# Attention rewritten: token-major queries, joined softmax weights, an fp32 V product, all query units ahead of the first score

## The chip, the cores and the metric

The kernel runs on one core of one Trainium2 chip. The metric is device time in microseconds (us): the median of several runs. The engines in the text are TensorE (PE, its weight loads PEld), VectorE (DVE), ScalarE (ACT), GpSimd (POOL) and SyncE (SP, which issues the loads). They run their own instruction lists in order and meet only at semaphores (`wait_ge`).

## The reference

A two-layer decoder trunk on 512 tokens of 1024 features, all float32: a gated short convolution layer, then one layer of differential attention, each with a squared-ReLU MLP. The change lies in the attention. Cut to it:

```python
def diff_attention(h, k, v, w_q, q_norm, lq1, lk1, lq2, lk2, sub_norm, w_o, lam_init):
    q = rms_norm((h @ w_q).reshape(b, s, N_HEADS, 2, HEAD_DIM), q_norm)   # 8 heads, 2 x 64
    lam = ...                                                              # a scalar
    for i in range(s // Q_BLOCK):                                          # 4 blocks of 128 rows
        sc = jnp.einsum('bqhcd,bkhcd->bhcqk', qb, kb) * HEAD_DIM ** -0.5
        p = jax.nn.softmax(jnp.where(causal, sc, NEG_INF), axis=-1)
        a = p[:, :, 0] - lam * p[:, :, 1]
        outs.append(jnp.einsum('bhqk,bkhe->bqhe', a, vb))                  # V_DIM = 128
    o = rms_norm(jnp.concatenate(outs, axis=1), sub_norm) * (1.0 - lam_init)
    return o.reshape(b, s, N_HEADS * V_DIM) @ w_o
```

## The kernel before

**Products.** Every large product is made of three fp32r matmuls: high part times high part, high times low, low times high. ACT makes the high part of a weight slab (`split`, L775) and DVE the low part (L1031). A slab is 512 KB of weights, loaded by SP into one of two raw buffers, and its two parts lie in rings of four. A slab is 24 matmuls of 512 columns (`product`, L436).

**Order.** First layer, its MLP, then 16 slabs of K and V (L585, token-major: four token blocks share a slab), with K normed and transposed head by head (`transpose_k`, L564). Then attention over 8 heads, the output projection (8 slabs), and the second MLP.

**Attention.** Queries are projected feature-major, one slab per head, and two heads ahead: `project` is cut in three pieces, which stand in PE's list between the groups of the head at work. The scale of the queries' norm is not applied to q: sums of q² are made on PE (`head_sums`, L599), POOL takes the power (L367), and exp gets it as its scale, with a bias that DVE makes from the row maximum (L1254, L1256). Each head has four block rows. For each: `scores` (L615, six matmuls, with a mask added at L618), row maximum on DVE, two exps on ACT (L918), the joined weights on DVE in three operations (L1264, L1266, L1268: both softmaxes are scaled, then added), transposes on PE (`weights_T`, L628), and a split of the transposed weights in high part (ACT, L926) and low part (DVE, L1273). The V product (`values`, L642) takes two block rows together, feature-major, in three fp32r terms. Then sums of o² on PE (`out_sums`, L649), the power on POOL (L375), a spread of the scale over the partitions on PE (`out_spread`, L461), the product on DVE (L1284), high part on ACT (L947) and low part on POOL (L400). POOL also makes the low parts of K (L384) and V (L396). Six pieces of the output projection fill PE's list in the last two heads.

Of the kernel before, what the change touches and what calls it, by code (L numbers as in the profile page):

```python
# [19 lines left out]
F32 = mybir.dt.float32  # L20
# [6 lines left out]
P = 128  # L27
T = 512
# [17 lines left out]
B_Q, B_AT, B_O, B_BC = 4, 5, 6, 7  # L46
HEAD_AHEAD = 2
Q_BANK = (B_AT, B_Q)
KV_BANKS = 6
K_T_AFTER = 7  # L50
# [25 lines left out]
def slot(n):  # L76


    return (n % 2) if S_Q <= n < S_WO else n % RING


def freed(n):

    if S_Q + 2 <= n < S_WO + 2:
        return n - 1
    return n - RING + 1 if n >= RING else 0
# [5 lines left out]


def heads(engine, head):


    head(0, 0, None, 1, 2)
    head(1, 1, 0, 2, 3)
    with engine.Fori(0, (H - 4) // 2) as it:
        head(it * 2 + 2, 0, it * 2 + 1, it * 2 + 3, it * 2 + 4)  # L100
        head(it * 2 + 3, 1, it * 2 + 2, it * 2 + 4, it * 2 + 5)
    head(H - 2, 0, H - 3, H - 1, None)
    head(H - 1, 1, H - 2, None, None)


def build(nc, x, a_norm, a_w_in, a_conv, a_w_out, kv_norm, w_kv, k_norm, b_norm, w_q, q_norm,
          lam_q1, lam_k1, lam_q2, lam_k2, sub_norm, w_o, mlp_norm, w_up, w_down, out):
    with ExitStack() as ctx:
# [21 lines left out]
        comp2 = sb("comp2", [P, 2])  # L130
# [12 lines left out]
        qms = sb("qms", [P, 2, 8])  # L143
        qpw = sb("qpw", [P, 8])
        k_ms = sb("k_ms", [P, 2, 32])
        k_rs = sb("k_rs", [P, 2, 32])
        q_scale = sb("q_scale", [P, 2, 2 * TB])
        oms = sb("oms", [P, 8])
        ors = sb("ors", [P, 8])
        nmax = sb("nmax", [P, 2, 2])  # L150
        bias = sb("bias", [P, 2, 2])
        rsum = sb("rsum", [P, 2, 2])
# [9 lines left out]
        p_buf = [work[:, (4 + 2 * i) * T:(6 + 2 * i) * T].rearrange("p (c k) -> p c k", c=2) for i in range(2)]  # L162
        at_hi = [ah[:, 0, :].rearrange("p (j q) -> p j q", j=2), ah[:, 2:4, :].rearrange("p a (j q) -> p (a j) q", j=2)]
        at_lo = [ah[:, 1, :].rearrange("p (j q) -> p j q", j=2), ah[:, 4:6, :].rearrange("p a (j q) -> p (a j) q", j=2)]
        q_hi, q_lo = [ah[:, 6 + 2 * b, :] for b in range(2)], [ah[:, 7 + 2 * b, :] for b in range(2)]
        k_hi, k_lo = [ah[:, 10 + 2 * b, :] for b in range(2)], [ah[:, 11 + 2 * b, :] for b in range(2)]
        v_hi, v_lo = ah[:, 14, :].rearrange("p (t e) -> p t e", t=TB), ah[:, 15, :].rearrange("p (t e) -> p t e", t=TB)
# [6 lines left out]
        sq_q = [work[:, T:2 * T], work[:, 3 * T:4 * T]]  # L174
# [39 lines left out]
        s_kT = sem("s_kT")  # L214
        s_kg = sem("s_kg")
        s_qsq = sem("s_qsq")
# [15 lines left out]
        s_Thi = sem("s_Thi")  # L232
        s_Tlo = sem("s_Tlo")
# [25 lines left out]
        def _(sp):  # L259
# [62 lines left out]
            for h in range(H):  # L322
                load(S_Q + h, cols(wq_d, h))
# [11 lines left out]
        def _(pool):  # L335
# [1030 lines left out]
```

## Time and profile before

| what | value |
|---|---|
| median of 3 runs | 1162.5 us (1161.51 to 1162.87) |
| profiled execution | 1161.75 us, span 1160.0 us |
| granted TensorE clock, mean | 0.999 of full |
| PE busy | 1148.7 us (99%) |
| DVE busy | 632.7 us (55%) |
| ACT busy | 383.2 us (33%) |
| POOL busy | 119.0 us (10%) |

The span goes from the first to the last instruction on the chip. Busy time is summed over instructions of an engine; matmuls overlap one another, so a matmul's own duration is longer than the distance from its start to that of the next.

### The profile page before, as it was taken

The numbers are of one execution on the slowest core, as the hardware profiler recorded it, in microseconds if no ns is written. First come the engines' busy times: TensorE is split into PE (matmuls) and PEld (weight loads), VectorE is DVE, ScalarE is ACT, GpSimd is POOL, SyncE is SP. The second block draws the span as 40 slices with busy tenths as digits, with TensorE's granted clock in tenths as the row PEclk, the third lists the DMA queues.
The fourth block names the chain that finished last, engine by engine and source line by source line (L and its number), as shares of the span: only waits on it lengthen the run. The fifth ranks groups of instructions, "written<-read, shape, count | busy, mean of one in ns | idle before, by whom it ended". The sixth has DMA issues, their size and how long they took to land.

```text
span 1160.0 us, 14437 instructions
## 1 busy us (share of the span) xinstructions
PE 1148.7 (99%) x5448; PEld 948.8 (82%) x5448; DVE 632.7 (55%) x871; ACT 383.2 (33%) x591; POOL 119.0 (10%) x94
## 2 busy tenths in 40 slices
PE   9999999999999999999999999999999999999998
PEld 7788888888888888888888788788888888888887
DVE  5765654733633633655543799946644544544542
ACT  6222133321321321334432677734321221222221
POOL 0000012000000000012210355424000000000000
PEclk9999999999999999999999999999999999999999
DMA  7333333333333333333222101113333233233232
GB/s 182 92 101 104 91 94 106 91 104 96 92 103 97 90 101 97 91 91 110 91 91 73 56 24 32 37 54 99 103 109 109 73 109 109 72 108 109 73 97 85
DMA packets 203109, 105.77 MB, mean 91 GB/s; under 512 B 12592, under 2 KB 198960, under 8 KB 203056
## 3 DMA queue, kind: packets, MB, share of 16 engines
q1 hardware_dynamic: 202016, 105.03, 31.7%
q8 instruction: 36, 0.59, 0.2%
q10 hardware_dynamic: 1040, 0.00, 0.0%
q14 instruction: 17, 0.14, 0.0%
HBM read 102.93 MB, written 2.10 MB: 91 GB/s over the span
## 4 chain that ended last, share of the span: by engine, by line
PE 95%; DVE 2%; issue 1%; DMA 1%; ACT 1%; SPq 0%; ACTq 0%; DVEq 0%
PE ps L436 81%; PE ps L585 8%; PE ps L615 1%; PE ps L642 1%; PE ps L461 1%; PE ps L628 1%; DMA kv<-in_x 1%; PE ps L649 0%; PE ps L618 0%; PE ps L599 0%; DVE nmax L1254 0%; DVE work L1266 0%; PE ps L564 0%; DVE ah L1273 0%; PE ps L553 0%
## 5 line engine op out<-in xcount | busy, mean ns | idle before, releaser
L436 PE MATMUL ps<-h,w_hi 128*128 128x512 f32 x1792 | 556.0, 391 | 1.7 <-DVE w_lo L1031 1.7
L436 PEld LDWEIGHTS ps<-h,w_hi 128*128 128x128 f32 x1792 | 333.3, 188 | 69.9 <-issue 1.6
L436 PE MATMUL ps<-h,w_lo 128*128 128x512 f32 x896 | 349.1, 390 | 0.0
L436 PE MATMUL ps<-ah,w_hi 128*128 128x512 f32 x1024 | 316.0, 390 | 0.0
L775 ACT ACTIVATE w_hi<-w_raw 128x1024 fp32r<-128x1024 f32 x184 | 192.4, 1052 | 253.4 <-DMA w_raw<-in_w_up 113.7
L1031 DVE TENSOR_TENSOR w_lo<-w_raw,w_hi 128x1024 fp32r<-128x1024 f32 x184 | 231.6, 1262 | 55.2 <-ACT w_hi L775 54.4
L436 PEld LDWEIGHTS ps<-ah,w_hi 128*128 128x128 f32 x1024 | 191.8, 188 | 39.8
L436 PE MATMUL ps<-ah,w_lo 128*128 128x512 f32 x512 | 199.3, 389 | 0.0
L436 PEld LDWEIGHTS ps<-h,w_lo 128*128 128x128 f32 x896 | 168.2, 188 | 35.5
L1042 DVE TENSOR_TENSOR xT<-ps,xT 128x512 f32<-128x512 f32 x80 | 55.3, 691 | 205.3 <-PE ps L436 205.3
L854 ACT ACTIVATE ah<-work 128x512 fp32r<-128x512 f32 x64 | 40.5, 633 | 238.8 <-DVE work L1138 238.8
L436 PEld LDWEIGHTS ps<-ah,w_lo 128*128 128x128 f32 x512 | 96.1, 188 | 19.9
L1138 DVE SCALAR_TENSOR_TENSOR work<-ps,rB 128x512 f32<-128x512 f32 x64 | 44.2, 691 | 124.0 <-PE ps L436 118.1
L355 POOL TENSOR_TENSOR work<-work 128x512 f32<-128x512 f32 x24 | 32.2, 1343 | 504.8 <-ACT work L784 504.8
L585 PE MATMUL ps<-w_hi,h 128*128 128x512 f32 x256 | 81.5, 393 | 0.0
L585 PEld LDWEIGHTS ps<-w_hi,h 128*128 128x128 f32 x256 | 48.1, 188 | 9.9
L585 PE MATMUL ps<-w_lo,h 128*128 128x512 f32 x128 | 49.8, 389 | 0.0
L1143 DVE TENSOR_TENSOR ah<-work,ah 128x512 fp32r<-128x512 f32 x64 | 44.4, 693 | 2.7
L1140 DVE TENSOR_TENSOR work<-work 128x512 f32<-128x512 f32 x64 | 44.3, 692 | 2.2
L778 ACT ACTIVATE h<-xT,gains 128x512 fp32r<-128x512 f32 x32 | 23.0, 720 | 65.1 <-DVE xT L1042 65.1
L918 ACT ACTIVATE work<-ps,bias,q_scale 128x128 f32<-128x128 f32 (+3 forms) x64 | 39.2, 627 | 4.2 <-DVE bias L1256 4.2
L1036 DVE SCALAR_TENSOR_TENSOR h<-xT,gains,h 128x512 fp32r<-128x512 f32 x32 | 24.0, 750 | 20.7 <-ACT h L778 20.7
(114 smaller groups left out, 655.1 us busy)
## 6 DMA issues: line engine op xcount, KB each, us to landing
w_raw<-in_w_up SPq DMA_DIRECT2D x64, 512.0 KB, 4.0
w_raw<-in_w_down SPq DMA_DIRECT2D x64, 512.0 KB, 3.8
w_raw<-in_a_w_in SPq DMA_DIRECT2D x23, 512.0 KB, 3.7
w_raw<-in_w_kv SPq DMA_DIRECT2D x16, 512.0 KB, 3.5
w_raw<-in_a_w_out SPq DMA_DIRECT2D x8, 512.0 KB, 3.9
w_raw<-in_w_q SPq DMA_DIRECT2D x8, 512.0 KB, 3.9
w_raw<-in_w_o SPq DMA_DIRECT2D x8, 512.0 KB, 4.0
kv<-in_x SPq DMA_DIRECT2D x4, 512.0 KB, 6.6
```

What stands on the lines that cost most here:

```text
L355: nc.gpsimd.tensor_tensor(sqsum, sqsum, sqb[m % 2], ALU.add).then_inc(s_add, 1)
L436: last = nc.tensor.matmul(ps[:, bank, :], w[:, s, k * P:(k + 1) * P], src(half, k), start=(k == 0 and i == 0), stop=(k == KC - 1 and i == 2))
L585: last = nc.tensor.matmul(ps[:, use % KV_BANKS, :], h2[:, half, k, t * P:(t + 1) * P], w[:, s, k2 * T:(k2 + 1) * T], start=(k == 0 and i = ...
L775: nc.scalar.activation(w_hi[:, slot(n), :], w_raw[:, n % RAW, :], ACT.Copy).then_inc(s_whi, 1)
L854: nc.scalar.activation(ah[:, jj, :], mix[jj % 2], ACT.Square).then_inc(s_ahi, 1)
L918: nc.scalar.activation(p_buf[i % 2][:, c, 0:kw], ps[:, 2 * (i % 2) + c, 0:kw], ACT.Exp, bias=bias[:, i % 2, c:c + 1], scale=q_scale[:, b, ...
L1031: V.tensor_tensor(w_lo[:, slot(n), :], w_raw[:, n % RAW, :], w_hi[:, slot(n), :].bitcast(F32), ALU.subtract).then_inc(s_wlo, 1)
L1036: V.scalar_tensor_tensor(h_of[i][:, 1, m, :], xT[:, m, :], gains[:, g, m:m + 1], h_of[i][:, 0, m, :].bitcast(F32), ALU.mult, ALU.subtract) ...
L1042: V.tensor_tensor(xT[:, m, :], ps[:, bank, :], xT[:, m, :], ALU.add).then_inc(s_acc, 1)
L1138: V.scalar_tensor_tensor(mix[j % 2], ps[:, (ubase + j) % ACC, :], 0.0, rB[:], ALU.max, ALU.mult).then_inc(s_r, 1)
L1140: V.tensor_tensor(mix[2], mix[j % 2], mix[j % 2], ALU.mult).then_inc(s_acc, 1)
L1143: V.tensor_tensor(ah[:, 8 + j, :], mix[2], ah[:, j, :].bitcast(F32), ALU.subtract).then_inc(s_alo, 1)
```

## The change

Queries are now made like K: token-major. The eight units are 2 groups of four heads times 4 token blocks. The first four (group 0) share four slabs like a fifth and sixth group of K and V would (`n` from 16 to 19), the last four are projected by `project(u, ks)` right behind, all ahead of `scores(0)`. For each unit ACT copies and squares it (`take_q`), DVE sums the squares along the row (`q_stats`), POOL takes the power, DVE multiplies (`q_norm_part`), PE transposes (`queries_T`), and ACT and DVE make high and low part (`q_hi`, `q_lo`) in `h2`. Between the pieces of units 4 to 7 stand the transposes of units 0 to 5.

The low parts of K for all heads are made by DVE in the K/V stage. The exps have scale 1.0 and the negative row maximum as bias. The joined weights are p1 + p2 x (-lambda x sum1 / sum2): two small operations and one over the row; the missing factor 1/sum1 cancels in the output's norm, whose epsilon is multiplied by sum1² (`oeps`). The transposed weights are evacuated once (`evacuate`, fp32). The V product is fp32, one block row at a time and token-major, so sums of o² are a row reduction on DVE (`out_ms`), the scale is a row operand (`out_norm`), and the output is transposed on PE (`out_T`) before its parts are made (`out_hi` on ACT, `out_lo` on DVE). Each step of PE's list handles the scores two block rows ahead. Chunks of the output projection (`WO_FILL`) stand in the steps of heads 3 to 7, and its first four slabs are split within heads 2 to 5 (`WO_EARLY`). The loop over heads is written out.

```diff
+B_AT, B_O, B_T, B_Q = 4, 5, 6, 7
 KV_BANKS = 6
+Q_BANK = (4, 5, 0, 1, B_Q, 2, 3, B_Q)
+QT_BANK = (B_T, B_O, B_T, B_O, B_T, B_O, B_T, B_T)
+STEPS = 4 * H
+WO_FILL = {(3, 1): (0,), (3, 2): (1,), (4, 1): (2,), (5, 1): (3,), (6, 1): (4,), (7, 1): (5,)}
+WO_EARLY = {(2, 3): 0, (3, 3): 1, (4, 2): 2, (5, 2): 3}
 K_T_AFTER = 7
 X_BANK = (4, 5, 6, 7, 2, 3, 4, 5)
 WO_BANK = (B_Q, 1, 2, 3, 0, 1, 2, 3)
@@ -74,33 +77,16 @@
 
 
...
-            def head(h, b, prev, nxt, far):
-                scores(h, 2, b)
...
-                if far is not None:
-                    project(far, b, range(0, 3))
...
-                if prev is not None:
-                    values(prev, 1)
-                weights_T(h, 0)
...
+            for u in (4, 5):
+                project(u, range(0, 2))
+                queries_T(2 * u - 8)
+                project(u, range(2, 5))
+                queries_T(2 * u - 7)
+                project(u, range(5, KC))
+            for u in (6, 7):
+                project(u, range(0, 3))
+                queries_T(u - 2)
+                project(u, range(3, KC))
+            scores(0)
+            queries_T(6)
+            scores(1)
+            for n in range(STEPS):
+                h, i = divmod(n, 4)
+                if n + 2 < STEPS:
+                    scores(n + 2)
+                if (h, i) == (3, 1):
+                    pe.wait_ge(s_qsq, 16)
+                if (h, i) in WO_FILL:
+                    project_out(0, WO_FILL[h, i])
+                if (h, i) == (H - 1, 2):
+                    pe.wait_ge(s_exp, 2 * STEPS - 2)
+                    project_out(1, range(0, 3))
+                if (h, i) == (H - 1, 3):
+                    project_out(1, range(3, 5))
+                if n:
+                    values(n - 1)
+                if n == 0:
+                    queries_T(7)
+                if i == 3 and h:
+                    out_T(h - 1)
+                weights_T(n)
+
+            pe.wait_ge(s_exp, 2 * STEPS)
+            project_out(1, range(5, 6))
+            project_out(2, range(0, 2))
+            values(STEPS - 1)
+            project_out(2, range(2, 6))
+            project_out(3, range(0, 6))
+            for m in range(ACC):
+                project_out(m, range(6, 7))
+            out_T(H - 1)
+            for m in range(ACC):
+                project_out(m, range(7, 8)).then_inc(s_used, 1)
...
+            def values(n):
+
+                h, i = divmod(n, 4)
+                pe.wait_ge(s_ev, n + 1)
...
                 for j in range(i + 1):
+                    last = nc.tensor.matmul(ps[:, B_O, i * P:(i + 1) * P], a_T[n % 2][:, j * P:(j + 1) * P],
+                                            v_all[:, j, h * P:(h + 1) * P], start=(j == 0), stop=(j == i))
                 last.then_inc(s_pv, 1)
...
+            def exps(m):
+
+                h, i = divmod(m, 4)
+                b = m % 2
+                act.wait_ge(s_mx, m + 1)
+                if m >= 2:
+                    act.wait_ge(s_at, m - 1)
+                else:
+                    act.wait_ge(s_qn, 2 * m + 6)
...
+            exps(0)
+            q_hi(6)
+            for n in range(STEPS):
+                h, i = divmod(n, 4)
+                if n + 1 < STEPS:
+                    exps(n + 1)
+                if i == 0 and h:
+                    copy_o(h - 1)
+                if n == 0:
+                    q_hi(7)
+                evacuate(n)
+                if i == 3 and h:
+                    out_hi(h - 1)
+                if (h, i) in WO_EARLY:
+                    split(S_WO + WO_EARLY[h, i])
...
+                if n > K_T_AFTER:
+                    h = n - K_T_AFTER - 1
+                    dve.wait_ge(s_khi, h + 1)
+                    V.scalar_tensor_tensor(ah[:, 8 + h, :], ps[:, BC + h % 2, :], hgs[:, 1:2], ah[:, h, :].bitcast(F32),
+                                           ALU.mult, ALU.subtract).then_inc(s_kg, 1)
...
+            for n in range(STEPS):
+                h, i = divmod(n, 4)
+                if i == 0 and h >= 2:
+                    out_lo(h - 2)
+                if n + 2 < STEPS:
+                    row_max(n + 2)
+                if i == 1 and h:
+                    out_ms(h - 1)
+                if n + 1 < STEPS:
+                    weights(n + 1)
+                if i == 2 and h:
+                    out_norm(h - 1)
+                if n == 0:
+                    q_lo(7)
+                if (h, i) in WO_EARLY:
+                    split(S_WO + WO_EARLY[h, i])
+            out_lo(H - 2)
             out_ms(H - 1)
             out_norm(H - 1)
+            out_lo(H - 1)
```

## Rows read from the trace of the kernel before

**Rows 1.** Windows: busy us (instructions) per engine, then granted TensorE clock, DMA
```profile
590.00:630.80 40.80, 40.80 (x192) 33.69 (x191) 13.92 (x17) 12.68 (x17) 7.97 (x3) 1.00 0.30 94
630.80:802.00 171.20, 167.41 (x1057) 135.78 (x1056) 133.55 (x265) 102.08 (x242) 71.47 (x53) 1.00 0.15 44
672.30:687.60 15.30, 15.30 (x111) 12.65 (x111) 14.55 (x31) 11.05 (x29) 8.35 (x6) 1.00 0.13 36
```

**Rows 2.** Timeline of PE in one head: start, us, engine, line, operation, count
```profile
671.40 1.11 PE L461 MATMUL ps<-ident,ors 128*128 128x128 f32 x8
672.35 0.60 PE L628 MATMUL ps<-ident,work 128*128 128x128 f32 x4
672.88 0.79 PE L615 MATMUL ps<-ah 64*128 64x384 f32 x6
...
673.72 1.00 PE L599 MATMUL ps<-comp,work 128*128 128x2 f32 x8
674.59 0.70 PE L436 MATMUL ps<-h,w_hi 128*128 128x512 f32 x2
...
676.76 1.59 PE L642 MATMUL ps<-ah 128*128 128x256 f32 x12
678.19 0.27 PE L628 MATMUL ps<-ident,work 128*128 128x128 f32 x1
678.39 0.96 PE L615 MATMUL ps<-ah 64*128 64x512 f32 x6
...
679.38 0.71 PE L436 MATMUL ps<-h,w_hi 128*128 128x512 f32 x2
...
681.55 0.95 PE L649 MATMUL ps<-ones,work 128*128 128x2 f32 x8
682.36 0.41 PE L628 MATMUL ps<-ident,work 128*128 128x128 f32 x2
682.71 0.62 PE L615 MATMUL ps<-ah 64*128 64x256 f32 x6
...
683.36 0.70 PE L436 MATMUL ps<-h,w_hi 128*128 128x512 f32 x2
```

**Rows 3.** Timeline of PE in the last four slabs of the output projection
```profile
780.10 0.74 PE L436 MATMUL ps<-h,w_hi 128*128 128x512 f32 x2 [0.43 <-DVE w_lo L1031]
...
801.35 0.61 PE L436 MATMUL ps<-h,w_hi 128*128 128x512 f32 x2
```

**Rows 4.** Timeline of DVE in the same head
```profile
677.89 1.23 DVE L1289 TENSOR_TENSOR w_lo<-w_raw,w_hi 128x1024 fp32r<-128x1024 f32 x1
679.03 0.16 DVE L1264 RECIPROCAL rinv<-rsum 128x2 f32<-128x2 f32 x1
679.23 0.41 DVE L1266 TENSOR_SCALAR work<-work,rinv,lams 128x256 f32<-128x256 f32 x1
...
680.28 1.21 DVE L1254 TENSOR_REDUCE nmax<-ps 128x2 f32<-128x1024 f32 x1
...
684.30 0.41 DVE L1254 TENSOR_REDUCE nmax<-ps 128x2 f32<-128x256 f32 x1
...
685.62 0.75 DVE L1268 SCALAR_TENSOR_TENSOR work<-work,rinv 128x512 f32<-128x512 f32 x1
```

**Rows 5.** Timeline of ACT in the same head
```profile
672.09 0.69 ACT L900 ACTIVATE ah<-ps,hgs 128x512 fp32r<-128x512 f32 x1
...
682.82 0.39 ACT L926 ACTIVATE ah<-ps 128x256 fp32r<-128x256 f32 x1 [1.19 <-PE ps L628]
683.10 0.77 ACT L918 ACTIVATE work<-ps,bias,q_scale 128x512 f32<-128x512 f32 x1
...
683.85 0.78 ACT L918 ACTIVATE work<-ps,bias,q_scale 128x512 f32<-128x512 f32 x1
```

**Rows 6.** Timeline of POOL in the same head
```profile
678.04 2.57 POOL L367 TENSOR_TENSOR qpw<-qms,mhalf 128x8 f32<-128x8 f32 x1 [0.66 <-DVE qms L1232]
...
684.46 1.64 POOL L375 TENSOR_TENSOR ors<-oms,mhalf 128x8 f32<-128x8 f32 x1 [1.35 <-DVE oms L1280]
```

More of the change, by code:

```diff
@@ L566, in transpose_k @@
                 last.then_inc(s_kT, 1)
[L569 removed]
+            for n in range(20):
                 g, kk = n // 4, n % 4
@@ L667, in project_out, with out_T @@
+            def out_T(h):
+                pe.wait_ge(s_on, h + 1)
+                if h:
+                    pe.wait_ge(s_lo, 8 * I_O + h)
+                else:
+                    pe.wait_ge(s_qlo, 8)
+                for i in range(TB):
+                    last = nc.tensor.transpose(ps[:, B_T, i * P:(i + 1) * P], o_sb[:, i * P:(i + 1) * P], ident[:])
+                last.then_inc(s_oT, 1)
+            def project_out(m, ks):
                 if 0 in ks:
                     wait_slab(S_WO + m)
-                return product(bank, S_WO + m, operand(I_O), ks, chunks_of(I_O))
@@ L903, in _ @@
-            act.wait_ge(s_kg, H)
-            act.wait_ge(s_kT, H)
-            for h in range(2):
-                k_hi_part(h, h)
-            act.wait_ge(s_used, S_Q + 1)
-            take_q(0, 0, Q_BANK[0], sq_q[0])
-            split(S_Q + 2)
-            def exps(h, i, b):
-                act.wait_ge(s_mx, h * 8 + 2 * i + 2)
-                if not (at_start(h) and i < 2):
-                    act.wait_ge(s_T, h * 4 + i - 1)
+                    nc.scalar.activation(ah[:, h, :], ps[:, BC + h % 2, :], ACT.Copy, scale=hgs[:, 1:2]).then_inc(s_khi, 1)
@@ L989, in _ @@
-            exps(0, 0, 0)
-            act.wait_ge(s_used, S_Q + 2)
-            take_q(1, 1, Q_BANK[1], sq_q[1])
-            heads(act, head)
+                act.wait_ge(s_oT, h + 1)
+                nc.scalar.activation(h2[:, 0, h, :], ps[:, B_T, :], ACT.Copy, scale=hgs[:, 2:3]).then_inc(s_hi, 1)
+            for n in range(16, 20):
+                split(S_KV + n + AHEAD)
+            split(S_Q + 6)
+            for u in range(3):
+                take_q(u)
+            split(S_Q + 7)
+            take_q(3)
@@ new lines, in _ @@
+            for n in range(16, 20):
+                split(S_KV + n + AHEAD)
+            split(S_Q + 6)
+            q_stats(0)
+            q_stats(1)
+            q_stats(2)
+            q_norm_part(0)
+            split(S_Q + 7)
+            q_norm_part(1)
+            q_stats(3)
+            q_lo(0)
+            q_norm_part(2)
+            q_lo(1)
+            q_norm_part(3)
+            q_lo(2)
+            q_stats(4)
+            q_lo(3)
+            q_norm_part(4)
+            q_stats(5)
```

578 lines of the change are left out of this document (217 added, 361 removed).

## The prediction

> **What bounds the kernel now.** I read the windows first: they say whose time a change in this stretch is. TensorE (PE) is busy 40.8 of 40.8 us ahead of the stretch that changes, and in that stretch, 630.8 to 802.0 (first query projection to last output projection), 167.4 of 171.2 us, at full clock, the higher of its two levels (2.4 GHz) [rows 1]. One head takes 15.3 us, with PE busy for all of it, VectorE (DVE) for 14.6, ScalarE (ACT) for 11.1. So PE's list of work sets the end today, with DVE just behind it and 3.8 us of waits in all. Then the timeline of PE in one head [rows 2]: to be seen there is that every attention group (scores, transposes, V product) stands between groups of L436, which are the projection of the head after next. That projection is the cover for every softmax wait. The change takes PE work away and takes that cover away too, so both lists have to be worked out.
>
> **Prices on PE** (start to next start) [rows 2]. The last four slabs of the stretch, 96 matmuls, run from 780.10 to 802.03 (their last three start at 801.35) [rows 3]: 21.93, less 0.1 for the start, is 5.45 for 24 matmuls, one slab or unit, and 0.68 for three, a chunk. Scores of one block row: 0.65 for 256 columns, 0.84 for 384 (672.88 to 673.72), 0.99 for 512 (678.39 to 679.38), so a head is 0.65+0.65+0.84+0.99 = 3.1. Transposes of four blocks 0.53, two 0.35, one 0.20; a head's ten 1.5.
>
> **Removed from PE, per head:** sums of q² (L599) 0.87, sums of o² (L649) 0.81, the spread of the output scale (L461) 0.95, together 2.6. The V product (L642), three fp32r terms, is 1.43 for the second pair of block rows and about half for the first: 2.15.
> **Added, per head:** four transposes of queries 0.55, four of outputs 0.55. The fp32 V product is 10 products of 128x128. No row has it, but L461 is the same form, fp32 against fp32 at 128x128, four products in 0.95, so 0.24 each: 2.4. The lower bound is the price of a transpose, 0.13 (1.3 a head). The upper one is two records of 0.27 that don't overlap (the lone one at 678.19): 0.54, 5.4 a head, which would put PE at 10.6 and above everything found below. I take 2.4, since L461 shows eight such records in 1.11.
> PE's list falls by 2.6+2.15-1.1-2.4 = 1.25 a head, 10 us in all. If PE stayed fully busy, that would be the gain.
>
> **What hides nothing any more.** The 192 query matmuls (43.6 us) now all stand ahead of the first score. In a head PE keeps 3.1+1.5+2.4+0.55 = 7.6 us. DVE [rows 4], where the next operation starts up to 0.09 before the end of the one before it and a dependent small one 0.20 after its start: row maxima, between the rows by size, 0.33+0.60+0.87+1.13 = 2.9; each step reciprocal 0.20, a small product 0.20 and the joining operation (0.67 for 512, by size 0.27, 0.40, 0.53) = 3.5; output statistics 0.95, output scale 0.6, output low part 0.67: 8.6. ACT [rows 5]: an exp of 512 columns is 0.75 to the next, taken as 0.1 less for each 128 columns fewer: twice 0.75+0.65+0.55+0.45 = 4.8; evacuations, the 0.28 of 256 columns with 0.1 a block more or less, 1.3; o and o² 1.0; high part 0.69 less an overlap of 0.11: 7.6. So no engine's own sum is over 8.6; the ring through them can be longer. I follow it in program order, each link from its start to when the next can start (handing over 0.05, as from the transposes' end at 682.77 to ACT at 682.82 [rows 2, 5], taken as 0.06; 0.14 where PE restarts and loads its operand first, an estimate):
> row maximum of (h+1,0) 0.33; weights of (h,3) 1.07; `out_norm` 0.69; to PE 0.14; `out_T` 0.55, which stands ahead of `weights_T(h,3)` 0.60; to ACT 0.06; evacuation 0.48; `out_hi` 0.57, which stands ahead of the exps of (h+1,1) 1.23; to PE 0.14; scores (h+1,3) 1.19; to DVE 0.06; row maximum of 1024 columns 1.13; `out_ms` 0.88; weights of (h+1,2) 0.94; and back. Sum 10.06 us a head. A second path (`out_hi`, `out_lo`, row maximum (h,2), weights (h,1)) is only 0.1 shorter, so both would have to shrink. The six chunks of `WO_FILL` (0.68 each) fall into PE's 2.4 us idle per head and cost under 0.1.
>
> **The stretch after, in order** (us from 630.8).
> 1. Eight units of projection 43.6; six query transpose groups among them 0.55 and 0.1 for each change of form, 3.9; one wait of 0.2 for the first normed queries: 47.7. (The 0.1 is an estimate: the pair of matmuls at 674.59, right behind another form, shows 0.70, and not the 0.61 that a pair within a stream has [rows 2, 3].) Their conversions (copy 0.5, square 0.6, reduction 0.7, power 1.64, product 0.75, about 5.5 in all) lie under two units of matmuls.
> 2. The opening: behind the last projection come its copy and square 1.25, reduction and scale 0.9, power 1.64 [rows 6] and handing over, product 0.75, as `exps(1)` waits for the eighth normed unit (its buffer lies over q_raw of units 6 and 7). Then DVE, in order, weights (0,0) 0.67, maximum 0.87, weights 0.81, last q low part 0.67, maximum 1.13, weights 0.94, PE and ACT 1.0 to the first exp of head 1: 10.7 in all. This is the largest new wait: PE has only 2 score rows for 4 us.
> 3. Head 1, which has no `out_T` of an earlier one in front: 9.1 (ring less 0.83 at most, up to the whole ring). Heads 2 to 6: 5 x 10.06 = 50.3.
> 4. Splits of the output weights in heads 2 to 5 (L1031 takes DVE 1.15, its ACT part 1.0 goes first). Behind step (h,3) ACT's part delays the exps and DVE waits for it with `out_lo` and a row maximum queued behind: 2.1 each, two of them; behind (h,2) they fit: 0.1. Together 4.3.
> 5. Head 7 to its last weight transposes 13.2 (a period, 2.2, and 0.9 as chunks of the output projection stand ahead).
> 6. Tail: 21 chunks of three matmuls 14.3; V product 1.0; `out_T` 0.55; then nothing is left for PE until high and low part of head 7 are there, 0.14+0.69+0.06+0.75 = 1.6; the wait for the fifth slab 0.43 as today [rows 3]; four slabs 21.8: 39.7.
> Sum 47.7+10.7+9.1+50.3+4.3+13.2+39.7 = 175.0, against 171.2: **+3.8 us**. The K split moves from POOL to DVE (8 x 0.67 in the K/V stage), where DVE is busy 13.9 of 40.8 us [rows 1]: nothing; without cover 5.4. Loads: the same eight 512 KB slabs of w_q, earlier; their queue is SP's and it waits only for splits. Nothing behind 802.0 changes. The profiled execution took 1161.75 us (span 1160.0), so it would take 1165.6; against the median 1162.5 it is 1166.3. I round up to 1167, since a ring followed misses handovers more often than it invents them.
>
> **A rule weighed.** POOL's power at 684.46 to 686.10 did not hold up DVE, whose two-input operation started at 685.62 and took its usual 0.75; the one at 678.04 took 2.57 in place of 1.64, started under a two-input DVE operation that ended at 679.12 [rows 4, 6]. The Trainium skill, "SBUF — State Buffer", section "SBUF: two separate sides", says that a DVE operation with two SBUF inputs and a GpSimd operation that reads SBUF exclude each other for the whole instruction, whoever starts first. The second pair agrees, the first doesn't.
>
> **Rivals.**
> A. *The power blocks DVE.* If it holds DVE's joining operation, which before met it only once a head, weights (h,2) wait up to 1.3 us for it (it starts 0.06 behind `out_ms`, the operation 0.4 later): 7 x 1.3 = +9, 1176. The rule of the Trainium skill just told would give this. The pair at 685.62 speaks against it [rows 4, 6]. 7%.
> B. *The clock falls.* PE will idle in every head, in pieces of 0.3 to 1 us and 2.4 in the opening, where now it idles nearly never; the profile has granted full clock everywhere [rows 1], with PE never under 97% busy, so it shows nothing for this case. At the lower level (1.2 GHz) PE's 7.6 would be 15.2, more than the ring: +5 a head, +30 to +40, 1195 to 1200. The Trainium skill, "TensorE: Matmul & The Clock Gate", section "A second HAM failure mode: psum-queue depth-cycling", tells of a kernel whose small idle pieces between matmul groups made the clock go to and fro; no row here can show it. As PE stays three quarters busy: 8%.
> C. *The other side: the ring closes tighter.* If handing over overlaps better than single durations say, DVE's own 8.6 becomes the limit: 6 x 1.46 = 9 less, and splits cost 2 less. It decides from a ring of 9.0 on (3.8 - 6 x 1.0 = -2.3): 1154 to 1160. For it: the engines' pitches are 0.1 to 0.2 under their durations. Against: I took pitches already. 17%.
> D. *Longer ring or opening* (11 us a head, each step losing 0.2 more): 1172 to 1180. 18%.
> E. *The forecast*, 1161 to 1172: 50%.
>
> **The numbers.** A measurement of this kernel can tell about 0.2% (2.3 us) from no change. Faster by over that (below 1160.2): nearly all of C, 0.16. Same (1160.2 to 1164.8): a third of E, 0.18. Slower: the rest, 0.66. The range leaves out B and the far end of C: 1157 to 1180; E's own is 1161 to 1172.
>
> **What would show it.** Queries: no DVE or ACT wait costs PE over 1 us before unit 7 ends (near 678.5). Then an idle piece of about 2.4 us on PE ended by the last queries' product, head distance 10 us (starts of the exps of (h,0)), PE busy about 76% in it, DVE about 90%, clock 1.00; V product matmuls at 0.12 a record; PE idle about 1.6 us ahead of the last chunks. Wrong, if the head distance is under 9.2 or over 11, if the clock row is under 0.95, or if a DVE operation doubles under the power.

## The result, and the profile after

The changed kernel takes 1164.8 us (median of 8 runs, 1164.51 to 1166.82), the kernel before, beside it on the same chip, 1162.2 (8 runs): a ratio of 1.0025, 95% interval 1.0016 to 1.0035. Its profiled execution has a span of 1162.6 us, 2.6 more than before; the forecast for the stretch was +3.8. So the change makes the kernel slower by a quarter of a per cent: little, but the interval lies clear of 1.

The windows of the changed kernel: first the projection of all query units, then one window for each of heads 0 to 6, cut where the first exp of a head starts on ACT, then head 7 with the output projection. Columns as in [rows 1].

```profile
630.80:678.86 48.06, 47.96 (x231) 39.09 (x231) 26.43 (x41) 18.01 (x27) 12.47 (x7) 1.00 0.21 66
678.86:688.66 9.80, 8.00 (x54) 5.51 (x54) 8.90 (x21) 6.49 (x21) 1.64 (x1) 0.83 0.00 1
688.66:697.49 8.83, 7.66 (x66) 5.62 (x62) 7.71 (x20) 6.69 (x24) 1.01 (x1) 1.00 0.01 2
697.49:707.53 10.04, 8.55 (x70) 6.11 (x66) 8.69 (x22) 7.27 (x25) 1.01 (x1) 1.00 0.01 2
707.53:719.65 12.12, 9.71 (x76) 7.21 (x72) 9.82 (x23) 8.43 (x26) 1.01 (x1) 1.00 0.17 45
719.65:732.72 13.07, 10.00 (x81) 7.53 (x77) 10.78 (x24) 9.37 (x26) 1.01 (x1) 1.00 0.14 41
732.72:742.88 10.16, 8.81 (x71) 6.62 (x69) 9.83 (x23) 8.32 (x25) 1.01 (x1) 1.00 0.18 53
742.88:752.09 9.21, 7.84 (x63) 5.76 (x61) 8.88 (x22) 7.37 (x25) 1.01 (x1) 1.00 0.21 59
752.09:804.60 52.51, 50.31 (x259) 41.11 (x256) 28.39 (x46) 22.80 (x47) 10.57 (x9) 1.00 0.14 41
sum 173.80, PE 158.84 PEld 124.56 DVE 119.44 ACT 94.73 POOL 30.71; mean PE 17.65 PEld 13.84 DVE 13.27 ACT 10.53 POOL 3.41
```

PE was busy 167.4 of 171.2 us in this stretch before [rows 1] and is now busy 158.8 of 173.8. So the work removed is really gone (8.6 us; the prediction had 10), but PE's idle time grew from 3.8 to 15.0. The waits of PE, changed kernel, from 590 to 810 us (who waits, for whom, us in all, times, longest) say for whom:

```profile
PE ps L612 <- DVE kv L1197: 7.2, 8, 1.3
PE ps L600 <- ACT kv L861: 3.6, 8, 1.1
PE ps L385 <- DVE h L1218: 1.6, 1, 1.6
PE ps L579 <- DVE work L1161: 1.5, 1, 1.5
PE ps L385 <- DVE w_lo L953: 0.4, 1, 0.4
```

L612 is `weights_T` and waits for the joined weights on DVE, L600 is `scores` and waits until the exps have read the bank. These two come back in every head. The third line is the empty place before the last chunks of the output projection, the fourth the last queries' product ahead of head 1, the fifth the old wait of [rows 3].

What sets a head's length is on DVE, which has a single wait in head 2:

```profile
700.96 0.75 DVE L1218 SCALAR_TENSOR_TENSOR h<-ps,hgs,h 128x512 fp32r<-128x512 f32 x1 [1.03 <-ACT h L881]
```

This is `out_lo`, which waits for `out_hi` on ACT. From the joining operation over 512 columns (L1197) at 697.21 to that of the next head at 707.25 it is 10.04 us: this wait of 1.03, and 9.01 in which DVE's operations follow each other without one.

The windows above can mislead, since an early split moves their borders. Behind step (h,2) ACT makes the split's high part (1.05 us) just ahead of the first exp of head h+1, and that exp starts 0.95 later: one window looks too long and the next too short. Counted from one joining operation over 512 columns to the next (starts 697.21, 707.25, 719.37, 731.50, 741.65 and 751.81), heads 2 to 6 take 10.04, 12.12, 12.13, 10.15 and 10.16. So the 9.21 of head 6 is no faster head, and the 13.07 of head 4 no slower one than head 3.

The timeline of PE, changed kernel, at the places that the prediction named:

```profile
677.53 0.62 PE L600 MATMUL ps<-ah,h 64*128 64x256 f32 x6
...
679.72 0.79 PE L600 MATMUL ps<-ah,h 64*128 64x384 f32 x6
...
682.27 0.65 PE L579 MATMUL ps<-ident,work 128*128 128x128 f32 x4 [1.54 <-DVE work L1161]
...
690.97 1.11 PE L624 MATMUL ps<-kv,work 128*128 128x128 f32 x8
691.92 0.27 PE L612 MATMUL ps<-ident,kv 128*128 128x128 f32 x1
...
779.36 0.73 PE L385 MATMUL ps<-h,w_hi 128*128 128x512 f32 x2 [1.57 <-DVE h L1218]
...
782.79 0.74 PE L385 MATMUL ps<-h,w_hi 128*128 128x512 f32 x2 [0.42 <-DVE w_lo L953]
...
804.73 0.62 PE L385 MATMUL ps<-h,w_hi 128*128 128x512 f32 x2
```

The last unit is projected at 677.5, the second MLP starts at 804.73 (before: 802.03).

### The profile page after: what moved, and what is told of

It is laid out like the page before. It is cut to its first block, busy times and chain, and to the rows that moved or that the text cites. A ratio compares the mean times of both kernels' runs of the same rounds, so it can differ in the third digit from the quotient of the medians.

```text
span 1162.6 us, 13951 instructions
## 1 busy us (share of the span) xinstructions
PE 1138.6 (98%) x5336; PEld 936.5 (81%) x5336; DVE 623.3 (54%) x844; ACT 375.9 (32%) x583; POOL 75.1 (6%) x58
## 4 chain that ended last, share of the span: by engine, by line
PE 93%; DVE 4%; issue 1%; ACT 1%; DMA 1%; SPq 0%; POOL 0%; ACTq 0%; DVEq 0%
PE ps L385 78%; PE ps L537 9%; PE ps L561 2%; DVE nmax L1182 1%; PE ps L624 1%; PE ps L600 1%; DMA kv<-in_x 1%; PE ps L612 1%; DVE kv L1197 0%; DVE rinv L1192 0%; ACT w_hi L708 0%; DVE h L1218 0%; DVE osum L1203 0%; PE ps L636 0%; PE ps L513 0%
## 5 line engine op out<-in xcount | busy, mean ns | idle before, releaser
L385 PE MATMUL ps<-h,w_hi 128*128 128x512 f32 x1664 | 514.6, 390 | 3.2 <-DVE w_lo L953 1.7
L385 PEld LDWEIGHTS ps<-h,w_hi 128*128 128x128 f32 x1664 | 310.6, 188 | 67.8 <-DVE h L1218 1.8
L385 PE MATMUL ps<-h,w_lo 128*128 128x512 f32 x832 | 323.9, 389 | 0.0
L708 ACT ACTIVATE w_hi<-w_raw 128x1024 fp32r<-128x1024 f32 x191 | 200.0, 1053 | 267.6 <-DMA w_raw<-in_w_up 111.3
L953 DVE TENSOR_TENSOR w_lo<-w_raw,w_hi 128x1024 fp32r<-128x1024 f32 x191 | 240.4, 1261 | 56.2 <-ACT w_hi L708 55.3
L385 PEld LDWEIGHTS ps<-h,w_lo 128*128 128x128 f32 x832 | 156.2, 188 | 32.8
L537 PE MATMUL ps<-w_hi,h 128*128 128x512 f32 x320 | 101.2, 392 | 0.0
L537 PEld LDWEIGHTS ps<-w_hi,h 128*128 128x128 f32 x320 | 60.1, 188 | 12.4
L537 PE MATMUL ps<-w_lo,h 128*128 128x512 f32 x160 | 62.3, 389 | 0.0
L861 ACT ACTIVATE kv<-ps,nmax 128x128 f32<-128x128 f32 (+3 forms) x64 | 33.4, 534 | 5.2 <-DVE nmax L1182 2.9
```

What stands on the lines that cost most here:

```text
L385: last = nc.tensor.matmul(ps[:, bank, :], w[:, s, k * P:(k + 1) * P], src(half, k), start=(k == 0 and i == 0), stop=(k == KC - 1 and i == 2))
L537: last = nc.tensor.matmul(ps[:, use % KV_BANKS, :], tok[:, half, k, t * P:(t + 1) * P], w[:, s, k2 * T:(k2 + 1) * T], start=(k == 0 and i ...
L708: nc.scalar.activation(w_hi[:, slot(n), :], w_raw[:, n % RAW, :], ACT.Copy).then_inc(s_whi, 1)
L861: nc.scalar.activation(p_buf[b][:, c, 0:kw], ps[:, 2 * b + c, 0:kw], ACT.Exp, bias=nmax[:, b, c:c + 1], scale=1.0, accum_out=rsum[:, h % 2 ...
L953: V.tensor_tensor(w_lo[:, slot(n), :], w_raw[:, n % RAW, :], w_hi[:, slot(n), :].bitcast(F32), ALU.subtract).then_inc(s_wlo, 1)
```

## The experiments

All times are compared with the changed kernel's 1164.8; the kernel before took 1161.7 to 1162.5 beside them. "Head n" is the window from the first exp of head n to that of head n+1. Line numbers of the experiments' kernels shift by some lines against the changed kernel's.

**e1_splits: the late splits alone.**

```diff
-WO_EARLY = {(2, 3): 0, (3, 3): 1, (4, 2): 2, (5, 2): 3}
+WO_EARLY = {(2, 2): 0, (3, 2): 1, (4, 2): 2, (5, 2): 3}
```

> Only the place of two early splits of output weights moves, from step 3 to step 2 of heads 2 and 3. Theory 1, the ring (a chain through DVE, ACT and PE sets the length of a head, and what stands in it costs its own time): the heads that begin behind such a split, 12.1 and 13.1 us from first exp to first exp, lose 1 to 2 us each, so 2 to 4 us less than the changed kernel (about 1161 to 1163). Theory 2, PE's list (the sum of PE's work sets the time, the pieces of attention just cost more than priced): no change, within 0.5 us.

Measured: 1160.88 us (11 runs), 3.9 less than the changed kernel, and not to be told from the kernel before (ratio 0.9993, 0.9984 to 1.0002). Its windows for heads 2 to 5:

```profile
697.48:708.47 10.99, 9.51 (x78) 6.96 (x74) 9.64 (x23) 8.22 (x25) 1.01 (x1) 1.00 0.01 3
708.47:718.63 10.16, 9.51 (x74) 7.18 (x72) 9.83 (x23) 8.32 (x25) 1.01 (x1) 1.00 0.18 52
...
728.79:738.95 10.16, 8.80 (x71) 6.61 (x69) 9.83 (x23) 8.32 (x25) 1.01 (x1) 1.00 0.18 53
```

From joining operation to joining operation heads 2 to 6 take 10.05, 10.15, 10.17, 10.15 and 10.16 (the 10.99 of head 2 is the shifted border). So a split behind step (h,3) cost 2.08 (12.12 against 10.04), and one behind (h,2) costs 0.10 to 0.12. In the changed kernel the late one is to be seen on ACT, where it stands between `out_hi` and the exps of (3,1):

```profile
710.28 0.68 ACT L881 ACTIVATE h<-ps,hgs 128x512 fp32r<-128x512 f32 x1
710.85 1.06 ACT L708 ACTIVATE w_hi<-w_raw 128x1024 fp32r<-128x1024 f32 x1
711.80 0.47 ACT L861 ACTIVATE kv<-ps,nmax 128x256 f32<-128x256 f32 x1
```

and on DVE, which waits for this high part ahead of `out_lo`:

```profile
711.94 1.23 DVE L953 TENSOR_TENSOR w_lo<-w_raw,w_hi 128x1024 fp32r<-128x1024 f32 x1 [1.97 <-ACT w_hi L708]
```

The wait is 1.97 in place of 1.03, and the low part itself takes 1.14 to the next start: 0.94 + 1.14 = 2.08. Behind (h,2) the low part's 1.14 takes the place of the wait of 1.03, which leaves 0.11.

**e2_outT: one link of the ring moved.** The transposes of the output stood ahead of the weight transposes of the same step; here they stand behind.

```diff
+                weights_T(n)
                 if i == 3 and h:
                     out_T(h - 1)
-                weights_T(n)
```

> The transposes of the outputs of the head before stand behind the transposes of the last softmax weights, not ahead of them. Same work on every engine. Theory 1, the ring: the last weights of a head no longer wait for out_norm (0.69) and the four output transposes (0.55); about 1.0 us less per head where the ring sets it, 10.04 to 9.1, in all 4 to 6 us less than the changed kernel (1159 to 1161). Theory 2, PE's list: no change. Theory 3, DVE's sum sets the head (8.7 us busy of 10.04): at most 1 us less in all, since DVE has the same work.

Measured: 1162.86 us (11 runs), 1.9 less, under what was expected. Two windows, heads 2 and 5:

```profile
697.65:707.00 9.35, 8.07 (x70) 6.06 (x66) 8.70 (x22) 7.30 (x25) 1.01 (x1) 1.00 0.00 2
730.80:740.96 10.16, 8.84 (x72) 6.70 (x71) 9.83 (x23) 8.48 (x26) 1.01 (x1) 1.00 0.19 53
```

Heads 2, 3 and 4 are 0.69 shorter (12.37 and 11.43 in place of 13.07 and 12.12), so the link was in the ring: DVE's wait for `out_hi` in head 2 is 0.33, where it was 1.03. Heads 5 and 6 don't move: the split's low part fills the place of this wait, DVE's operations stand back to back, and its list is the limit there. The ring and DVE's list lie 0.1 apart, so to shorten one is worth nothing where the other stands.

**e3_nofill and e7_refill: work that was thought free to leave out.** In e3 the six chunks of the output projection in heads 3 to 7 are moved to the tail. e7 leaves three matmuls that nobody reads in each of the six places.

```diff
-                if (h, i) in WO_FILL:
-                    project_out(0, WO_FILL[h, i])
 ...
+            project_out(0, range(0, 6))      # in the tail
             pe.wait_ge(s_exp, 2 * STEPS)
             project_out(1, range(5, 6))
```

> The six chunks of the output projection that fill PE's list in heads 3 to 7 (0.68 us each) stand behind the heads. Theory 1, the ring: inside the heads they cost nothing, behind them their whole price, so 3.5 to 4.1 us more than the changed kernel (1168.3 to 1169), with frames of heads 3 to 7 unchanged within 0.2. Theory 2, PE's list: the heads get shorter by what the tail gets longer, no change.

Measured: 1172.0 us (5 runs), 7.2 more than the changed kernel. The longer tail explains 6 x 0.68 = 4.1 of it, and e7, which has the same tail, is indeed 4.0 slower than the changed kernel.

> As e3_nofill, the six chunks are computed behind the heads, but three matmuls of the same size stand again at each of their six old places (into the free bank, not part of the result). So PE has more work than in e3_nofill, and the tail is as long. Theory C (in e3_nofill the clock fell in heads 3 to 5 because PE idled more there, and that cost 3 of its 7 us): the clock stays at 1.00 and the time falls below e3_nofill though work is added, 1168.5 to 1169.5. Rival (the fill had another use, or the tail costs 7 us by itself): 1172 or more.

Measured: 1168.79 us (4 runs). e7 has 18 matmuls more than e3 and is 3.2 us faster. Heads 3 and 4 of e3, then of e7:

```profile
707.92:720.39 12.47, 10.05 (x68) 7.24 (x66) 10.18 (x23) 8.42 (x25) 1.01 (x1) 0.80 0.15 43
720.39:734.63 14.24, 11.86 (x75) 8.85 (x74) 10.64 (x24) 9.38 (x27) 1.01 (x1) 0.74 0.13 37
```
```profile
707.79:719.92 12.13, 9.72 (x76) 7.21 (x72) 9.84 (x23) 8.45 (x26) 1.01 (x1) 1.00 0.16 45
719.92:732.99 13.07, 9.99 (x81) 7.53 (x77) 10.77 (x24) 9.38 (x27) 1.01 (x1) 1.00 0.14 41
```

The third column from the end is the granted clock: 0.80 and 0.74 in e3 (and 0.94 in head 5, which took 11.03), 1.00 in e7. PE's timeline in head 3 of e3 shows what went before and what came of it:

```profile
713.26 0.96 PE L600 MATMUL ps<-ah,h 64*128 64x512 f32 x6 [1.12 <-ACT kv L859]
...
714.40 0.49 PE L624 MATMUL ps<-kv,work 128*128 128x128 f32 x2
716.04 0.69 PE L612 MATMUL ps<-ident,kv 128*128 128x128 f32 x2 [1.15 <-DVE kv L1195]
716.66 1.01 PE L600 MATMUL ps<-ah,h 64*128 64x256 f32 x6
```

PE is idle for 1.12 us, works for 1.6, is idle for 1.15, and then the scores of 256 columns take 1.01 where they take 0.62 [rows 2] at full clock: the lower level (1.2 GHz). In e7 the second piece is 0.61 long, and the clock stays up. The Trainium skill, "TensorE: Matmul & The Clock Gate", section "A second HAM failure mode: psum-queue depth-cycling", tells of small idle pieces that make the clock go to and fro. The trace of e3 agrees: the scores of 256 columns take 1.01 at 716.66 and again at 719.90, those of 384 columns take their usual 0.79 at 723.36, and at 729.94, behind the same two waits in head 4, 256 columns take 1.01 once more. So the chunks had no price as work, but they had a value that the prediction didn't name: they keep PE's clock up in heads 3 to 5.

**e4_dve: one operation more on DVE.** A second row maximum over the same bank in the fourth step of each head, into an array that nobody reads.

```diff
+                if m % 4 == 3:
+                    V.tensor_reduce(spare[:], ps[:, 2 * b:2 * b + 2, 0:kw], AX_X, ALU.max, negate=True)
                 V.tensor_reduce(nmax[:, b, :], ...)
```

> DVE repeats the row maximum of the widest scores of each head into a spare tile (1.13 us, eight times, not part of the result). Theory 1, the ring: that operation lies in the ring, so each head gets 1.0 to 1.2 us longer, in all 7 to 9 us more than the changed kernel (1172 to 1174). Theory 2, PE's list: DVE is busy 8.7 of 10.04 us and has room for it: under 1 us more.

Measured: 1182.18 us (4 runs), 17 more for 8 x 1.13 = 9 us of work. Heads 1 and 5 of e4:

```profile
689.90:699.85 9.95, 7.66 (x66) 5.69 (x62) 8.90 (x21) 6.79 (x24) 1.01 (x1) 0.99 0.01 2
740.13:753.37 13.24, 11.34 (x70) 8.85 (x70) 11.04 (x23) 8.43 (x26) 1.01 (x1) 0.76 0.14 40
```

Where the clock stays at full, the head is longer by just the operation (8.83 to 9.95, and head 3 from 12.12 to 13.26), so DVE is on the path. Where it falls to 0.76, the head is 3.1 longer (10.16 to 13.24). So of the 8 us beyond the operation's own, 5.6 lie in heads 2, 4, 5 and 6, the ones with a lower clock than before (0.87, 0.90, 0.76, 0.78).

**e9_fill2 and e10_fill1: filling PE's gaps.** e1_splits, with six matmuls of 512 columns that nobody reads in each of heads 1 to 6: in e9 right ahead of the weight transposes of (h,2), where PE waits for DVE; in e10 one step earlier.

```diff
+                if i == 2 and 1 <= h <= 6:       # e10: i == 1, behind the scores
+                    ...
+                    for j in range(6):
+                        nc.tensor.matmul(ps[:, B_T, :], h1[:, j % 2, 0, 0:P], h1[:, 0, 1, :], start=(j == 0), stop=(j == 5))
                 weights_T(n)
```

> e1_splits plus six matmuls of 512 columns that nobody reads, right ahead of the weight transposes of tile (h,2), in each of heads 1 to 6; they take a bank that the output transposes share. 6 by 0.22 = 1.3 us of TensorE in a head, 7.9 in all. Theory order (work put where TensorE waits for the normalised weights is free up to that wait): frames of heads 1 to 6 within 0.4 us of e1_splits' (8.82, 10.99, 10.16, 10.16, 10.16, 9.21), the run 1160.5 to 1163. Rival busy (TensorE's busy time decides now, so that each us put in costs a us): each frame 1.3 longer, the run 1168 to 1169.

> The same six matmuls in each of heads 1 to 6, one step earlier: behind the scores and the output projection's chunk of step (h,1), ahead of that step's weight transposes. Theory order: there they stand ahead of the ring's next link with no wait to fill, so each head is 0.8 to 1.3 longer, the run 1165.5 to 1168.5, while e9_fill2 isn't. Rival slack (the frame has room on TensorE, 8.6 busy of 10.0, so that it doesn't matter where the work stands): like e9_fill2, within 1 us of it.

Measured: 1161.96 and 1163.26 us (10 runs each), against 1160.88 without the 7.9 us of work: +1.1 and +2.4. Head 4 of e9:

```profile
719.57:729.73 10.16, 10.08 (x77) 7.62 (x75) 9.70 (x22) 8.44 (x25) 1.01 (x1) 1.00 0.18 53
```

PE is busy for 10.08 of 10.16 us and this head is not a tenth longer than in e1. PE's busy time alone doesn't set a head. It wasn't free everywhere: heads 1 and 3 took 9.35 and 10.79 (8.82 and 10.16 in e1), head 2 10.83 (10.99), and together that is the 1.1 us. The place matters, though by less than expected: a step too early costs 1.3 us more over six heads, and against e1 each of heads 3 to 6 is 0.56 to 0.59 longer in e10 (joining to joining) where 0.8 to 1.3 was expected, head 2 not at all. Most of the filler comes out of the waits that follow: from 697 to 750 us PE waits 4.9 us for the joined weights in e1; in e10 it waits 0.3 for them and 1.0 for the outputs' product.

**e5_inter, e6_all, e8_spread, e11_best: two query units taken out of the opening.** In all of them units 6 and 7 are projected in pieces within heads 0 to 3, so the first score comes 12 us earlier. e5 is e1 with that, e6 is e5 with e2's order, in e8 the pieces are smaller and later, and the first three chunks of the output projection stand later too, all in head 4; in e11 unit 7 is earlier again, the chunks are back in their places and the splits are as in e12 (below).

```diff
+Q_FILL = {(0, 0): (6, 0, 3), (0, 1): (6, 3, 5), (0, 2): (6, 5, 7), (0, 3): (6, 7, 8),
+          (1, 1): (7, 0, 2), (1, 2): (7, 2, 4), (2, 1): (7, 4, 6), (2, 2): (7, 6, 8)}
 ...
-            for u in (6, 7):
-                project(u, range(0, 3))
-                queries_T(u - 2)
-                project(u, range(3, KC))
 ...
+                if (h, i) in Q_FILL:
+                    u, k0, k1 = Q_FILL[h, i]
+                    project(u, range(k0, k1))
```

> Query units 6 and 7 (10.9 us of matmuls, with their transposes 12) are projected in eight pieces within heads 0 to 2 as PE's fill, and the scores start two units earlier; the early splits stand as in e1_splits. Work and forms are the same. Theory 1 (missing cover: PE's idle time in the heads comes from the ring and can take matmuls for nothing): the 12 us leave the stretch ahead, the opening wait on the last unit goes too (3), the units' DVE work (2.3 each) lengthens heads 1 and 2: 8 to 11 us less than e1_splits, 1150 to 1153, with the clock at 1.00 in head 0. Theory 2, PE's list: the same sum of PE work, so the same time as e1_splits within 1 us.

Measured: 1158.4 us (6 runs), ratio 0.9968 (0.9956 to 0.998). Faster than both kernels, but by 2.5 us against e1 where 8 or more were expected.

> e5_inter with the output transposes behind the last weight transposes of a head, as in e2_outT. Theory 1 with the split heads bound by DVE's own sum, as e2_outT showed (10.16 with and without): only heads without a split or a query unit gain 0.7, one or two of them, so 0.5 to 1.5 us less than e5_inter, 1149 to 1152. If the ring through out_norm sets every head: 4 us less.

Measured: 1158.11 us (5 runs), ratio 0.9964 (0.9951 to 0.9978). Its heads 0, 2 and 3:

```profile
666.34:679.15 12.81, 11.59 (x80) 8.68 (x78) 9.59 (x21) 7.47 (x23) 1.64 (x1) 1.00 0.00 0
...
691.05:702.81 11.76, 11.76 (x95) 9.58 (x92) 10.54 (x24) 8.91 (x27) 1.01 (x1) 1.00 0.01 1
702.81:715.72 12.91, 10.58 (x82) 8.04 (x80) 12.15 (x26) 9.86 (x28) 2.65 (x2) 1.00 0.15 42
```

The first exp starts at 666.34 in place of 678.92 in e1: 12.6 saved. Heads 0 to 3 take 49.4 in place of 39.7: 9.7 given back. The amount explains most of it. PE was idle for 1.8, 1.2, 1.5 and 0.7 us in e1's heads 0 to 3, 5.1 together, and two units bring 10.9 us of matmuls and 1.1 of transposes. So at best 12.6 - (12.0 - 5.1) = 5.7 could stay; 2.9 did.

> e6_all with the pieces of query units 6 and 7 spread wider: one or two chunks of a unit in a step of heads 0 to 3, a part of them right ahead of the weight transposes of tile (h,2), where the trace of after shows TensorE idle for 0.9 to 1.3 us, and the six chunks of the output projection moved back by up to two steps. Theory order (e6_all's heads 0 to 3 are long, 12.81, 11.90, 11.76 and 12.91 against 9.74, 8.82, 10.99 and 10.16 in e1_splits, because two or three chunks put into one step stand ahead of the ring's next link in TensorE's list): the same products in smaller pieces cost less; heads 0 to 3 together 43 to 46 instead of 49.4, the run 1152 to 1155. Rival amount (it's the work that counts, 16 chunks by 0.66 to 0.72 = 11 us of TensorE and 2.3 us of VectorE for each unit, wherever they stand): heads 0 to 3 stay within 1 us of 49.4 and the run within 1157 to 1159.

Measured: 1159.95 us (11 runs). Heads 1 and 3 fall to 10.38 and 10.15, but head 4 grows to 15.73, with PE waiting 1.38 for the low part of an output, whose bank the transposes take, then 1.82 for the low part of unit 7's queries, and the clock at 0.89:

```profile
716.37 0.63 PE L584 MATMUL ps<-ident,work 128*128 128x128 f32 x4 [1.38 <-DVE h L1232]
...
718.93 1.65 PE L605 MATMUL ps<-ah,h 64*128 64x512 f32 x6 [1.82 <-DVE h L1184]
```

Unit 7 was simply too late for the scores of tile (4,3).

> The order of e6_all with three changes: the pieces of query units 6 and 7 in steps of one or two chunks, part of them behind the transposes' wait as in e8_spread; unit 7 two steps earlier than there, so that the scores of tile (4,3) find it (in e8_spread they waited 2 us for it and head 4 took 15.7); and the four splits on GpSimd as in e12_pool. e8_spread's heads 0 to 3 took 12.81, 10.38, 11.75 and 10.15, and heads 5 and 6 10.16 and 9.22. If the 15.7 was nothing but the late unit: heads 0 to 3 12.8, 10.8, 11.5, 11.5, heads 4 to 6 9.3 each where the splits on GpSimd cost VectorE nothing: 74.5 in place of e6_all's 78.9, the run 1153 to 1155. If the unit's work itself costs what it cost e6_all wherever it stands, heads 0 to 3 take 49.4 together and the run is 1155.5 to 1157.

Measured: **1156.92 us** (5 runs), ratio 0.996 (0.9946 to 0.9974): 7.9 less than the changed kernel and the fastest of all. Heads 2 and 3:

```profile
689.63:702.04 12.41, 12.41 (x95) 9.95 (x92) 11.60 (x28) 8.90 (x27) 2.64 (x2) 1.00 0.00 1
702.04:714.93 12.89, 10.94 (x87) 8.59 (x85) 12.07 (x26) 9.85 (x29) 5.01 (x3) 1.00 0.15 42
```

In head 2 PE has no idle time left, in head 3 DVE is idle for 0.8. Heads 0 to 3 together took 48.5 against e6's 49.4: small pieces win 0.9 us, the amount stays. That is the second of the two cases of the expectation. Its 9.3 for heads 4 to 6 didn't come either; e12_pool shows why.

**e12_pool: the split's low half on another engine.** In e1's heads with a split DVE is busy 9.83 of 10.16 us, POOL 1.01.

```diff
 # POOL, behind out_power(h - 1)
+                if (h, 2) in WO_EARLY:
+                    n = S_WO + WO_EARLY[h, 2]
+                    pool.wait_ge(s_whi, n + 1)
+                    nc.gpsimd.tensor_tensor(w_lo[:, slot(n), :], w_raw[:, n % RAW, :], w_hi[:, slot(n), :].bitcast(F32),
+                                            ALU.subtract).then_inc(s_wlo, 1)
 # DVE
-                if (h, i) in WO_EARLY:
-                    split(S_WO + WO_EARLY[h, i])
```

> e1_splits with the low halves of the four early output-weight slabs made by GpSimd instead of VectorE (1.22 us less for VectorE in each of heads 2 to 5). In e1_splits VectorE is busy 9.83 of 10.16 in these heads, and the head without a split takes 9.21 at 8.88. Theory list (VectorE's own list is the bound of these heads): frames of 10.2 for head 2 and 9.2 to 9.4 for heads 3, 4 and 5, the stage 3 to 3.7 shorter, the run 1157.2 to 1158. Rival ring (the loop of waits through four engines takes about 10 us whoever does the split): frames stay within 0.3, the run within 1 us of 1160.9. Rival port (GpSimd's 1024-wide subtraction, some 2 to 2.5 us, holds up VectorE's operations with two inputs in SBUF while it runs): VectorE's operations beside it take visibly longer than 0.75 for 512 columns, and a good part of the gain is lost: heads of 9.6 to 10.2.

Measured: 1160.98 us (11 runs), the same as e1. The heads take 10.11, 10.12 and 10.13 where they took 10.16. POOL's subtraction in head 3, and what DVE did meanwhile:

```profile
709.31 2.36 POOL L368 TENSOR_TENSOR w_lo<-w_raw,w_hi 128x1024 fp32r<-128x1024 f32 x1 [2.10 <-DVE work L1219]
```
```profile
709.96 0.16 DVE L1195 RECIPROCAL rinv<-rsum 128x1 f32<-128x1 f32 x1
...
710.47 1.35 DVE L1202 SCALAR_TENSOR_TENSOR kv<-kv,rinv 128x128 f32<-128x128 f32 x1
711.74 0.74 DVE L1223 SCALAR_TENSOR_TENSOR h<-ps,hgs,h 128x512 fp32r<-128x512 f32 x1
```

The small operation ran beside it at its usual length, and so did the next one. The joining operation, which has two inputs in SBUF, took 1.35 in place of 0.35 and ended 0.15 behind POOL's. So 1.14 us left DVE's list, and 1.00 came back as a wait inside an instruction, where no list of waits shows it. That is the rule of the Trainium skill, "SBUF — State Buffer", section "SBUF: two separate sides", at work: the two exclude each other for the whole instruction. The trace agrees with it here, on its number.

But in e12 the block is not what keeps the head at 10.12. Here `out_hi` on ACT runs from 710.94 to 711.62, and `out_lo`, which needs it, starts at 711.74: without the block DVE would have stood waiting for ACT, as in the changed kernel's head 2, which has no split and takes 10.04. So e12 alone could have gained 0.1 a head at most. It is in e11_best, where e2's order has shortened the ring (9.35 in e2's head 2), that the block has a price. Head 6 of e11_best, first ACT, then DVE:

```profile
736.34 0.70 ACT L900 ACTIVATE h<-ps,hgs 128x512 fp32r<-128x512 f32 x1
```
```profile
736.52 1.35 DVE L1220 SCALAR_TENSOR_TENSOR kv<-kv,rinv 128x128 f32<-128x128 f32 x1
737.79 0.74 DVE L1241 SCALAR_TENSOR_TENSOR h<-ps,hgs,h 128x512 fp32r<-128x512 f32 x1
```

`out_hi` is done at 737.04, but DVE comes to `out_lo` only at 737.79, behind the joining operation that POOL holds up. The head takes 10.11 from joining to joining, 0.76 more than the 9.35.

## Why the prediction was right, step by step

1. *The projection*, 47.7 to the end of unit 7: measured 46.7 (630.8 to 677.5). The price of 5.45 a unit held; the supposed wait of 0.2 didn't come, and the transposes of queries were priced too high: the six among the projections take 0.35 to the next start (0.42 the first), not 0.55, which is 1.1 less. The 0.3 by which the two are more than the 1.0 missing wasn't followed.
2. *The opening*, 10.7: measured 11.1 (677.5 to 688.66), by the chain that was named. The wait for the last queries' product is 1.54 on PE; 2.4 was forecast, because two groups of scores were counted in front of it, where there are three (the third at 679.72, 0.84 with its mask).
3. *Heads*: head 1 8.83 for 9.1. Head 2, the only later one with no split in it, took 10.04 for the ring's 10.06. e2_outT showed that the front of this ring, which both paths of the prediction share, is on the path: taking out one link (0.55 with what goes with it) shortened the head by 0.69. But the path that closes it isn't the one that was named. The named one goes through the exps of (h+1,1) and the scores of (h+1,3). In head 2 these scores' last record ends at 703.07, while the row maximum over them starts at 703.39, right behind DVE's joining operation at 702.99. So the "second path" (`out_hi`, `out_lo`, row maximum, weights) ended last, about 0.3 later than the named one. The exps were priced too long: from the first one's start to the scores it is 1.08 (700.81 to 701.89), for 1.23 + 0.14. The weights were priced too short by 0.1 a step, as the small product takes 0.31 to the next start (702.68 to 702.99), not 0.20. The two errors go against each other, so the 0.02 between 10.04 and 10.06 is in part luck; the size of the ring isn't. In heads with a split behind (h,2) the place of DVE's wait is full and the limit is its own list, 10.16. Heads 2 to 6 together took 54.6, for 50.3 + 4.3.
4. *Splits*: 2.08 and 2.09 for the two behind (h,3), 0.11 and 0.12 for those behind (h,2), from joining to joining; forecast 2.1 and 0.1. e1_splits took just these out and was 3.9 faster. Without them the change would have made no difference that can be measured: of the 2.7 us by which the stretch grew, the splits behind (h,3) are more than all.
5. *Head 7* to its last transposes: 12.7 for 13.2. *Tail*: 40.0 for 39.7, with the waits of 1.57 (1.6) and 0.42 (0.43).

Sum 46.7 + 11.1 + 8.8 + 54.6 + 12.7 + 40.0 = 173.9, forecast 175.0. The measured median is 2.2 under the 1167.0: 1.1 from this sum, 0.3 as the kernel before was at 1162.2 in these runs, and 0.7 from rounding up for handovers that would be missed. None were missed, so the rounding was wrong.

*Sizes that were off, without a price:* PE was said to be busy 7.6 us in a head, and is 8.55 of 10.04 in head 2 (85% for 76%); the row adds up records, which end later than the next group could start. ACT was put at 7.6 (its terms add up to 7.7) and has 7.27. The fp32 product is 0.24 each, as taken (eight records from 690.97 to 691.92).

*Rivals.* A, the power on POOL that blocks DVE: false. Changed kernel, head 4, first POOL, then DVE:

```profile
729.79 1.01 POOL L355 TENSOR_TENSOR ors<-oms,mhalf 128x4 f32<-128x4 f32 x1 [11.12 <-DVE oms L1209]
```
```profile
730.13 0.62 DVE L1197 SCALAR_TENSOR_TENSOR kv<-kv,rinv 128x384 f32<-128x384 f32 x1
```

The joining operation starts under the power and takes its usual 0.62 (before it was 0.75 for 512 columns [rows 4], under the power of [rows 6]). e12_pool shows the block with a wide subtraction on POOL, so the rule holds for that one and not for a power on 4 columns; what makes the difference wasn't tried.
B, the clock: full in all heads but head 0 (0.83), where it costs under 0.1, as e7_refill has 1.00 there and the same head 0.06 shorter. Two of the prediction's own signs of being wrong did show: a clock row under 0.95, in head 0, which it hadn't looked at by itself, and a head distance over 11, in heads 3 and 4, where its own price for the late splits had it. And the margin is small: in e12_pool's profile head 0 had 0.68 and took 10.65 for 9.74, and e3 and e4 lost it in three or four heads by changes of a few us. 8% was little for a kernel so near to it.
C, a tighter ring (9.0): false, 10.04. D, a longer one: false.

## What to carry to other kernels

When work that covered a latency moves elsewhere, walk the ring of waits through all engines link by link, by distances from start to start, and add to it each operation that stands in a list between two links: here that gave a head of 10 us to about 0.3 us a path (and to 0.02 by luck), and showed two 1 us operations one step too late that cost 2.1 each. Two paths that close that near each other are to be priced with equal care. When windows are cut at an operation that a change can shift, cut them a second time at another. Before moving an operation to an idle engine, look at what it shares with the engine that it leaves, and before taking filler work off PE, look at the waits that it shortens: here one went from 0.62 to 1.15 us and the clock with it.

## What the runs showed of the hardware that was not expected

- More matmuls, less time: 18 matmuls whose result nobody reads kept the granted clock at 1.00 in heads 3 to 5, where it was 0.80, 0.74 and 0.94 without, and the program took 1168.8 us in place of 1172.0.
- A block by POOL lengthens the blocked instruction's own record (0.35 to 1.35 us) and raises DVE's busy time; it isn't among the waits. It costs nothing where the engine would have waited anyway (e12_pool), and about 0.7 us a head where not (e11_best).
- Exps are shorter than before: 0.69 for 512 columns against 0.78 [rows 5]. Their scale is now the constant 1.0 and no longer a column, and their output lies elsewhere; which of the two it is wasn't tried.
- A power on POOL takes 1.01 us for 4 columns and 1.64 for 8 [rows 6].
